# A fused two-block transformer kernel: when four modulation chunks, the bias table products and one low half are computed

## What is computed

```
sh1, sc1, ga1, sh2, sc2, ga2 = modulation(c, w_mod, b_mod)
u = (rmsnorm(x, g_mix) * (1 + sc1) + sh1) @ w_in
```

## Time and profile before

| | |
|---|---|
| time, median of 3 runs | 1880.05 us (1874.72 to 1881.85) |
| the profiled execution's own time | 1872.19 us |
| its span (first to last instruction) | 1870.2 us |
| mean granted TensorE clock | 0.956 of full |
| PE busy | 1717.7 us, 92% |
| DVE busy | 1073.4 us, 57% |
| ACT busy | 708.3 us, 38% |
| loaded by SP's queue | 293.98 MB |
| mean rate of all DMA | 165 GB/s |

### The profile page before, as it was taken

The page is one execution under the profiler, slowest core; times in us unless marked ns, Lnnn a source line. Parts: engine busy times, 40 slices in busy tenths (PEclk is TensorE's granted clock), DMA queues, the critical chain, the costliest instruction groups (busy, mean ns, idle before and its releaser), DMA issues.

```text
span 1870.2 us, 25835 instructions
## 1 busy us (share of the span) xinstructions
PE 1717.7 (92%) x10684; PEld 1390.9 (74%) x10684; DVE 1073.4 (57%) x1648; ACT 708.3 (38%) x892; POOL 83.9 (4%) x95
## 2 busy tenths in 40 slices
PE   4999988999999999998899997987999989879998
PEld 1786556777777777754589996665999766669996
DVE  2664556644444446854666676556666465566654
ACT  2323444421212124333444444364333344533332
POOL 0120000100000001100000001001000010010000
PEclk7999988999999999998989998988999999889999
DMA  9325970233333334368545554342555545335542
GB/s 349 113 86 212 356 249 5 109 135 135 135 136 135 135 135 152 110 241 301 180 158 185 194 192 174 118 176 83 177 187 172 186 167 183 110 113 181 180 171 100
DMA packets 172389, 309.20 MB, mean 165 GB/s; under 512 B 3281, under 2 KB 54737, under 8 KB 171633
## 3 DMA queue, kind: packets, MB, share of 16 engines
q1 hardware_dynamic: 168608, 293.98, 45.2%
q10 hardware_dynamic: 3376, 12.00, 1.7%
q0 software_dynamic: 288, 1.57, 0.2%
HBM read 305.44 MB, written 2.10 MB: 164 GB/s over the span
## 4 chain that ended last, share of the span: by engine, by line
PE 76%; DVE 12%; ACT 6%; DMA 3%; issue 2%; POOL 1%; DVEq 0%; ACTq 0%; POOLq 0%; SPq 0%
PE bank L584 57%; PE twin L584 16%; DVE ring_r L1270 4%; PE bank L593 3%; ACT arena_r L2079 3%; ACT arena L2079 2%; DMA ring<-in_w_mod 2%; DMA ring<-in_w_in 1%; DVE arena L1270 1%; POOL rs L2530 1%; DVE params L1270 1%; DVE arena L1915 0%; DVE X L1830 0%; DVE arena_r L1949 0%; DVE GA L1270 0%
## 5 line engine op out<-in xcount | busy, mean ns | idle before, releaser
L584 PE MATMUL bank<-arena_r 128*128 128x512 f32 (+2 forms) x2104 | 694.8, 377 | 14.5 <-DVE arena_r L1949 6.7
L1270 DVE TENSOR_TENSOR ring_r<-ring,arena_r 128x4096 fp32r<-128x4096 f32 (+4 forms) x99 | 394.4, 3984 | 195.5 <-ACT arena_r L2079 194.6
L584 PEld LDWEIGHTS bank<-arena_r 128*128 128x128 f32 x2104 | 401.4, 191 | 94.4 <-issue 8.3
L2079 ACT ACTIVATE arena_r<-ring 128x4096 fp32r<-128x4096 f32 (+4 forms) x99 | 324.1, 3274 | 360.1 <-PE bank L584 140.0
L584 PE MATMUL twin<-actT_r,arena_r 128*128 128x256 f32 x1440 | 264.2, 284 | 4.1 <-DVE arena L1352 2.2
L584 PE MATMUL bank<-ring_r,arena_r 128*128 128x512 f32 x624 | 246.2, 395 | 0.0
L584 PEld LDWEIGHTS twin<-actT_r,arena_r 128*128 128x128 f32 x1440 | 226.4, 193 | 5.5 <-issue 2.7
L584 PE MATMUL bank<-arena_r,actT_r 128*128 128x512 f32 (+3 forms) x616 | 214.3, 379 | 8.6 <-DVE ring_r L1270 3.2
L2079 ACT ACTIVATE arena<-bank 128x512 f32<-128x512 f32 (+6 forms) x190 | 90.3, 475 | 326.1 <-PE bank L584 275.8
L584 PE MATMUL twin<-actT_r,ring_r 128*128 128x256 f32 x736 | 208.7, 284 | 0.0
L584 PE MATMUL bank<-ring_r,actT_r 128*128 128x512 f32 (+3 forms) x488 | 179.4, 368 | 0.0
(11 more groups left out here) (206 smaller groups left out, 1681.4 us busy)
## 6 DMA issues: line engine op xcount, KB each, us to landing
ring<-in_w_mod SPq DMA_DIRECT2D x24, 2048.0 KB, 9.2
ring<-in_w_ada SPq DMA_DIRECT2D x24, 2048.0 KB, 8.2
ring<-in_w_gate_up SPq DMA_DIRECT2D x44, 1024.0 KB, 7.6
ring<-in_w_down SPq DMA_DIRECT2D x20, 2048.0 KB, 7.7
ring<-in_w_up SPq DMA_DIRECT2D x16, 2048.0 KB, 7.8
ring<-in_w_in SPq DMA_DIRECT2D x12, 2048.0 KB, 8.5
ring<-in_w_out SPq DMA_DIRECT2D x8, 2048.0 KB, 8.8
ring<-in_w_down SPq DMA_DIRECT2D x8, 1792.0 KB, 7.5
```

Of the source, the lines that this page charges most:

```text
L584: ins = nc.tensor.matmul(out_, lhsT, rhs, start=start, stop=stop)
L1270: return v.tensor_tensor(o, x, y, op)
L2079: return nc.scalar.activation(o, x, func, **kw)
```

## The change

Four places of `loads()` and of the PE program, and one of the DVE program. The number of loads, of fills, of matmuls and of DVE operations is the same in all.

- Layer 1 of the first trunk: one modulation chunk is loaded between the first two `up1` chunks, and its `fill()` stands behind the out projection, ahead of `normed`.
- Both layers of the second trunk: the last of the four fills, in step 7 of the attention loop, goes. In layer 0 it comes back behind the out projection, and its chunk is loaded between the first and the second `up2` chunk. In layer 1 nothing comes back, as the count has moved on by one.
- Beginning, PE: one fill, two table products, one fill, two table products, a wait for the high half of the first `w_in` chunk, two fills.
- Beginning, DVE: the low half of that chunk is made behind the table and ahead of `mod_columns(0)`.

```
@@ loads()
         for q in range(4):
             for kind in ("up1", "down1"):
                 out += [(kind, l, 2 * q + i) for i in range(2)] + take(1 if l == 0 else 0)
+                if l > 0 and q == 0 and kind == "up1":
+                    out[-1:-1] = take(1)
     for l in range(L):
         ins = [("in2", l, c) for c in range(len(CH2))]
-        out += [("par2a", l, 0)] + ins[:3] + [("par2b", l, 0)] + take(1) + ins[3:] + take(3)
+        out += [("par2a", l, 0)] + ins[:3] + [("par2b", l, 0)] + take(1) + ins[3:] + take(2)
         out += [("out2", l, h) for h in range(2)]
-        out += [("up2", l, c) for c in range(F2 // 256)]
+        out += [("up2", l, 0)] + take(1 if l == 0 else 0) + [("up2", l, c) for c in range(1, F2 // 256)]
@@ PE, layer1
                 else:
+                    fill()
                     normed(tiles1(l), 2 * l + 1)
@@ PE, layer2, attention loop
-                    if j in (AHEAD + 2, AHEAD + 3):
+                    if j == AHEAD + 2:
                         fill()
@@ PE, layer2, behind the out projection
                 mark["y", l, 1] = k["v"]
+                if l == 0:
+                    fill()
                 normed([0, 1], 2 * (L + l) + 1)
@@ PE, beginning
-            for _ in range(NFIRST - 1):
+            for pair in range(2):
                 fill()
-            for h in range(4):
-                b, filled = take("v")
-                mm(b[:, :], t5col[:, h, :], t5hot, inc=filled)
-            fill()
+                for h in (2 * pair, 2 * pair + 1):
+                    b, filled = take("v")
+                    mm(b[:, :], t5col[:, h, :], t5hot, inc=filled)
+            pe.wait_ge(whi_ready, 1)
+            for _ in range(NFIRST - 2):
+                fill()
             mod_columns(0)
@@ DVE, layer1
                 if l == 0:
-                    split([("in1", 0, 0)])
                     turned([0, 1, 2, 3], act_lo, act_lo_r)
-                if l == 0:
                     handed.append(("t5",))
@@ DVE, beginning, behind the table
+            split([("in1", 0, 0)])
             mod_columns(0)
             modulate(0, 0)
```

## The result

The changed kernel takes 1892.8 us (median of 5 runs, 1887.21 to 1895.35), the kernel before in the same series 1879.04 us (5 runs, 1873.3 to 1881.85). The ratio is 1.0063, 95% interval 1.0042 to 1.0085: slower by 11.8 us, between 7.9 and 16. The forecast was 1888, range 1880 to 1896.

The account below looks back on a forecast made before the run. PE was taken to bound the kernel, three quarters of its chain. Terms -2.6 - 1.7 - 2.8 + 10.4 + 4.4 = +7.7 us gave 1887.8 from the 1880.05 median, said as 1888, range 1880 to 1896.

Parts of the forecast that it names:

- The ring: First down1 and third up2 chunks load a stage later; PE stalls 5.3 and 5.1 us, together +10.4.
- Rival A: At the first down1 and third up2, the late chunk is not late enough; only gains, -7.1: 1873. Chance 0.10.
- Clock behind the stalls: PE runs at 0.50 behind both new stalls, costing 2.2 us each, +4.4, ends 3.4 and 6.0.
- Rival B: PE returns at 2.4 GHz behind the out projections, giving back 3.0 + 2.5 us: 1882.3. Chance 0.12.
- The covered fills: Two fills behind out projections fit in PE's idle time: cost 0, up to 1.9 us each if landing late.
- The beginning: DVE's low half leaves the chain, -2.6 us; PE's reordered fills and tables, -1.7 us.
- The loops: One fill leaves each second-trunk attention loop; 1.4 of its 1.9 us gained in each, -2.8, ends 0 and -3.8.
- rival D: Gains stay away: no clock rise at the beginning, loops' gain taken by ACT's and DVE's chain; 1892.6. Chance 0.16.
- Rival C: In one of the two late-chunk places a further chunk is late, with its clock, +7.5: 1895. Chance 0.10.

Follow-up runs that it names:

- noload: Changed kernel without loading the two modulation chunks behind out projections; their fills read the out projection's chunk instead: ratio 0.9976 to the kernel before, -4.5 us.
- nowork: Changed kernel, both loads kept, fills behind out projections cut to 32 of 512 columns (first trunk eight matmuls, second four): ratio 1.004 to the kernel before, +7.5 us.
- second_trunk: Kernel before, one fill moved from the attention loop of the second trunk's layer 1 to behind its layer 0's out projection: ratio 1.0057, +10.7 us.
- begin_pe: Kernel before with PE's part of the beginning alone, DVE's low half left where it was: ratio 1.0001, +0.2 us.
- begin_in2: Kernel before with both beginning edits, and the fourth in2 chunk of both second-trunk layers split in two parts: ratio 0.9952, -9.0 us.
- after_again: The changed kernel itself, run again on one chip beside the repeated narrow-fill kernel: ratio 1.0063 to the kernel before, +11.8 us.
- nowork_again: Changed kernel with both loads but narrow fills behind the out projections, repeated on one chip beside the changed kernel: ratio 1.0043 to the kernel before, +8.1 us.
- begin: Kernel before with only the two beginning edits, PE's and DVE's: ratio 0.998, -3.8 us.
- begin_dve: Kernel before with DVE's beginning edit alone, the first chunk's low half moved ahead of the columns: ratio 0.9989, -2.1 us.
- loops_narrow: Kernel before with step 7's fill in both second-trunk attention loops cut to 32 columns instead of 512, loads as before: ratio 1.0011, +2.1 us.
- halves: Changed kernel with the two late chunks (first down1, third up2) split in two parts each: ratio 1.0035 to the kernel before, +6.6 us.
- first_trunk: Kernel before, one fill moved from the attention loop of the second trunk's layer 0 to behind first trunk layer 1's out projection: ratio 1.0044, +8.3 us.

## Why the prediction was right, point by point

**The sign and the size.** Forecast +7.9 against the median, measured +11.8 (7.9 to 16), inside the range. Slower by over 0.5% had a chance of 0.42, within 0.5% one of 0.52: the likeliest class was the wrong one of the two, by 2.4 us. The forecast's own mechanism is what happened. That the number came so near rests in part on luck: the loops gave less than forecast and a term was missing, both towards slower, and the low clock cost less over a whole layer than right behind the stalls.

**The ring.** Taken 5.3 and 5.1; measured 5.2 and 6.05. The steps came as listed: 7.8, 3.63, 4.43 and then PE; 7.73, 3.63, 4.43, 0.43, 0.43. In the first the 0.42 for a bank did not come: PE followed DVE's low half, by 0.55. The second came out 0.9 longer, 0.6 of it in the way from issue to PE, 17.4 instead of 16.8 us: its load is issued in two parts, and the chain has the first part's issue of 0.41 in front of a landing of 7.73, where I had 7.9 for both; and the handovers between the engines, 0.02 to 0.14 each, make 0.36. The other 0.3 is a misreading: I took 1329.9, the start of ACT's operation in rows 12, for PE's end with the second chunk. PE's first matmul of the third chunk had started at 1329.40. In the kernel after PE was through 11.4 us behind the issue, not 11.7. Rival A, not late enough, is out: `noload` shows what it would have given, 0.9976 against 1.0063, some 16 us (and 12 less than `nowork` on the same chip).

**Clock behind the stalls.** Taken 2.2 each; measured right behind them 1.7 and 2.6. Of the first, 1.2 or more is still there when PE reaches layer 0's fourth `in2` chunk (210.2 to 211.8 us in the six executions with this stall, 208.4 to 209.0 in the seven without it and with that chunk unsplit). Of the second less is left at layer 1's: 219.6 to 220.9 us with it, 219.0 in `noload`, whose ring is shifted too. Seven of the eight executions without the second stall have a low clock of 3.4 us some 138 us behind the third `up2` chunk, none of the six with it has one. Between `noload` and the changed kernel the two differences are 1.8 and 0.7, so 2.5 of the 4.4 can be found in the stretch; this rests on one execution of each.

**Rival B,** PE back at the higher clock behind the out projection, is out: in all 14 executions the clock was at 0.50 when PE came back. In the profiles of before and after it stayed there as long behind 4.6 of idle as behind 6.5, 9.2 us. How long it stays is another matter: in four executions (second_trunk, begin_pe and begin_in2 behind 6.5, after_again behind 4.6) it was only 4.2 to 4.4. The Trainium skill (TensorE: Matmul & The Clock Gate, section Why this matters for your kernels) warns of idle between bursts; here the trace agrees for the stalls. At the fourth `in2` chunk the clock fell behind every wait of 3.12 us or more, stayed up behind those of 2.73 or less, and between them, 2.83 to 3.10, both happened (28 waits in 14 executions).

**The covered fills.** Taken 0. The stretch is the same with and without their work; the runs on one chip leave up to some 4 us open (`nowork_again`).

**The beginning.** Taken -4.3. The mark lies at 66.5, 66.7, 68.8 and 68.8 in the four executions without these edits, mean 67.7, and at 63.2 to 64.1 in the eight with both, mean 63.6: -4.1. The runs of `begin` say -3.8. How it divides is not shown. Against the same mean PE's edit alone moves the mark by 1.2 and DVE's alone by 0.6, less together than the two in one; but the four executions without either edit lie 2.4 apart, and the intervals of `begin_pe` (-2.8 to +3.2) and `begin_dve` (-6.6 to +2.3) hold both nothing and the terms I took.

**The loops.** This is the term that was mis-sized, while the sign and the mechanism of the whole held: "I take 1.4 of the 1.9 in each loop: -2.8". The 1.35 at equal clock is right. It is not what the kernel gets: layer 0 gives back 1.1 in a longer low clock, and `loops_narrow` as a whole measured +2.1 (-2.3 to +6.2). By the traces -1.6 is left of the 2.8, and the runs' interval doesn't reach 2.8. This is rival D, in part of its half on the loops, with another cause than the one I gave: by these traces not ACT's and DVE's chain takes it, but the clock.

**What was not in the sum.** In layer 1 of the second trunk the stall at the fourth `in2` chunk is 3.71 instead of 2.68, with a low clock behind it, which the kernel before did not have. It is so in every kernel whose ring is shifted by a chunk at that point: 3.71, 3.66, 3.86, 4.05, 3.97, 3.66 and 3.91 (after, second_trunk, noload, nowork, halves, after_again, nowork_again), and where it is not, 2.68 before, 2.64 to 2.83 in first_trunk, begin_dve, loops_narrow and begin_pe, and 1.13 in begin. The load takes longer there, kernel before and kernel after:
```profile
1530.12 8.01 DMA ring<-in_w_in
```
```profile
1550.49 9.05 DMA ring<-in_w_in
```
So an added chunk has an effect a layer later, about 1 us and 1.7 of clock. Rival C, lateness passed on at once, is out: no further chunk was late behind either stall.

**The sum again:** beginning -4.1, stalls +11.3, clock behind them +4.3, layer 1's `in2` chunk +2.7, loops -2.7 and +1.1 back: +12.6, against +11.8. That they meet so closely says little. In the stretch these terms make +16.7, where the two profiled executions differ by 14.6: before has the low clock of 3.4 us behind the third `up2` chunk, worth 1.7, that after lacks, and the last part came out 0.6 shorter. With 14.6 the sum would be +10.5; the interval of the runs, 7.9 to 16, holds both.

## What to carry to other kernels

A free place on the compute engine is not yet a free place in the ring: a chunk added to a ring of three moves the next load but one a whole stage later, and if load and preparation together (16 us here) are longer than a stage (11), the difference stands on the path. Before moving work into a wait, write down for each load behind it which read frees its slot. And where a stall is load, one engine, another engine in a row, cutting the chunk in two is worth a trial before small work is moved about: for two chunks it took 4.7 us out of the stretch, where the move added 14.6.

## What the runs showed that was not expected

**The same program differs by up to 16.5 us in one stretch.** From the mark of the beginning to SP's first `w_out` load in layer 1 of the first trunk nothing is changed in any of these kernels. It takes 817.3 us in the kernel before and 826.4 in the one after, 818 to 829 in the other executions with both beginning edits, and up to 833.8 in second_trunk. PE's waits there, where I compared them (the first 350 us and the last 190), are the same ones; the number and place of the stretches at 0.50 differ from execution to execution. 9.1 of the 21.1 us between the two profiles are this, which is why the profiles overstate the change and why one profile of each can't give a total.

**One load lands later when the ring is shifted.** The fourth `in2` chunk of layer 1 takes 7.96 to 8.18 us in the seven executions where it goes to slot 0, and 8.98 to 9.39 in the seven where it goes to another. The slot alone doesn't explain it: in layer 0 the same kind of chunk takes 8.41 to 8.95 in slot 0 and 8.43 to 8.77 in slot 1. The cause is open; it was not tried.
